# Value products ahead of the turning of probabilities in a TensorE attention stream

## The reference

```
# NSA branch, 8 heads of 64, one shared K/V group; per block of 128 queries:
s = q . k / 8 - slope * dist ;  p = softmax(s, masked) ;  o = p @ v
o_cmp  : 32 compressed keys      o_sel : all keys of the selected 64-key blocks
o_win  : the last 512 keys       o_a = g0*o_cmp + g1*o_sel + g2*o_win
# differential branch, 4 heads, two maps each:
a = softmax(s_0) - lambda * softmax(s_1) ;  o_b = a @ v      (v has 128 columns)
```

## Time and profile before

| What | Value |
|---|---|
| Median of three runs | 2092.49 us |
| Span of the profiled execution | 2086.2 us |
| PE busy in that span | 1972.7 us (95%) |
| DVE, ACT, POOL busy | 1163.0, 678.2, 152.2 us |
| Attention block in the trace | about 696 to 1106 us |

### The profile page before, as it was taken

How to read it: one execution, slowest core, us unless ns; L and a number is a source line. 1 busy time by engine, 2 the same in 40 slices (tenths; PEclk the granted TensorE clock), 3 DMA queues, 4 the chain that set the end, 5 groups by cost and what they waited for, 6 DMA issues and landing times. The chain is left out here.

```text
span 2086.2 us, 34791 instructions
## 1 busy us (share of the span) xinstructions
PE 1972.7 (95%) x13032; PEld 1856.5 (89%) x13032; DVE 1163.0 (56%) x2531; ACT 678.2 (33%) x1273; POOL 152.2 (7%) x190
## 2 busy tenths in 40 slices
PE   5889999999997799999998999999999999999997
PEld 4658798789996688898898999999999999999997
DVE  4944333334244677777775546655556565555555
ACT  5623243331223566666573133311111110101011
POOL 1442100101300100000200000000000000000000
PEclk8799999999998899999899999999999999999999
DMA  9776453521001000000003541221212020211102
GB/s 311 255 215 205 152 180 98 156 94 60 30 26 66 1 1 1 1 1 1 1 1 102 173 131 50 62 61 30 60 30 60 30 60 30 60 31 59 40 0 82
DMA packets 151758, 157.10 MB, mean 75 GB/s; under 512 B 15859, under 2 KB 132483, under 8 KB 151604
## 3 DMA queue, kind: packets, MB, share of 16 engines
q1 hardware_dynamic: 140076, 130.73, 20.4%
q0 software_dynamic: 4656, 16.40, 2.3%
q10 hardware_dynamic: 6912, 8.46, 1.1%
HBM read 139.33 MB, written 18.32 MB: 76 GB/s over the span
## 5 line engine op out<-in xcount | busy, mean ns | idle before, releaser
L1877 DVE SCALAR_TENSOR_TENSOR l_x2T<-tail_bank,g_modT,l_x2T 128x344 f32<-128x344 f32 (+1 forms) x528 | 265.3, 566 | 101.5 <-PE tail_bank L1614 101.3
L1614 PE MATMUL tail_bank<-l_wo 128*128 128x344 f32 x1584 | 270.2, 319 | 1.8 <-DVE late_total_s L1883 1.8
L1614 PEld LDWEIGHTS tail_bank<-l_wo 128*128 128x128 f32 x1584 | 252.7, 188 | 2.0 <-issue 2.0
L1448 ACT ACTIVATE l_act<-tail_bank 128x344 f32<-128x344 f32 x66 | 30.2, 457 | 523.6 <-PE tail_bank L1596 523.6
L884 PE MATMUL nsa_out<-zs_z,nsa_probT 128*128 128x64 f32 (+1 forms) x1344 | 176.1, 277 | 5.3 <-DVE zs_z L1040 5.1
L884 PEld LDWEIGHTS nsa_out<-zs_z,nsa_probT 128*128 128x128 f32 x1344 | 169.1, 198 | 7.1 <-DVE zs_z L1040 7.0
L1596 PE MATMUL tail_bank<-late_words_hi,l_uhi 128*128 128x344 f32 x528 | 169.7, 321 | 3.3 <-DVE late_words_lo L1780 3.3
L1596 PE MATMUL tail_bank<-late_words_lo,l_uhi 128*128 128x344 f32 x528 | 169.3, 321 | 0.0
L1596 PE MATMUL tail_bank<-late_words_hi,l_ulo 128*128 128x344 f32 x528 | 169.2, 320 | 0.0
L1596 PE MATMUL tail_bank<-late_words_lo,late_wo 128*128 128x344 f32 x528 | 169.1, 320 | 0.0
L1596 PE MATMUL tail_bank<-late_words_hi,l_wo 128*128 128x344 f32 x528 | 169.1, 320 | 0.0
(11 more groups left out here) (504 smaller groups left out, 4329.2 us busy)
## 6 DMA issues: line engine op xcount, KB each, us to landing
mod_wr<-in_w_ada SPq DMA_DIRECT2D x24, 1024.0 KB, 5.3
kin_kin<-in_cache_kv SPq DMA_DIRECT2D x64, 256.0 KB, 3.4
late_gate<-in_w_ffn_in SPq DMA_DIRECT2D x22, 512.0 KB, 5.7
l_raw_o<-in_w_ffn_out SPq DMA_DIRECT2D x22, 512.0 KB, 3.6
late_raw<-in_w_ffn_in SPq DMA_DIRECT2D x22, 512.0 KB, 5.4
gate_d<-dec_gate ACTq DMA_DIRECT2D x48, 172.0 KB, 2.9
late_gate<-gate_d SPq DMA_DIRECT2D x8, 1032.0 KB, 5.5
dec_vin<-in_cache_kv SPq DMA_DIRECT2D x64, 128.0 KB, 2.2
```

The costliest lines, as they stand in the source:

```text
L1448: act.activation(sg[(j + c) % 2], pg[(j + c) % 2][:, 0:TCH], ACT.Silu).then_inc(silu_done, 1)
L1614: mm = pe.matmul(po[u % 4][:, 0:TCH], w[j][:, k * P:(k + 1) * P], a[j][:, tok(c)], start=(q == 0), stop=(q == 2))
L1877: mm = dve.scalar_tensor_tensor(out=here, in0=po[u % 4][:, 0:part_w(c)], scalar=g.modT[:, 5 * KD + k, NDEC:NC9], in1=here, op0=ALU.mult, o ...
```

## The change

In `follow`, PE issues the value products of the job five back first and the turning of the job four back second. Before it was the other way round. The conditions, the waits inside both functions, the semaphores and every other engine's stream are the same.

```diff
                 def follow(t):
+                    if t >= LAG + 1:
+                        values(t - LAG - 1)
                     if LAG <= t < NJ + LAG:
                         transpose_probs(t - LAG)
-                    if t >= LAG + 1:
-                        values(t - LAG - 1)
```

## The result

The kernel after takes 2120.05 us (median of four runs, 2117.34 to 2125.08), the kernel before 2089.16 in the same set: a ratio of 1.015, interval 1.0125 to 1.0176, so 31 us slower. A second set of six runs, beside 24 of before, gave 2118.84 against 2086.88, ratio 1.0146 (1.0123 to 1.017).

What follows compares the result with a forecast made beforehand. PE (TensorE) was taken to bound the attention stage. Uncovered copies 20.0, late exponentials 4.7, `out` bank 7.8, less 1.6, 1.5 and 2, clock 0, sum to +27.4 us; on 2092.5 that gives 2120 us, range 2103 to 2138.

Steps and rivals of the forecast that it cites:

- (i): Granted clock over the attention stage: more idle time may bring more slow stretches; bounds -5 and +16 us, taken as 0.
- (a): Attention steps with a copy of four tiles or longer before a one-tile score: 13 places, together 7.9 us.
- (b): Steps with one to three tiles before a score one tile longer, and three similar: 26 places, together 7.3 us.
- (d): Drain of the attention stage: the four last jobs lose their only cover, 0.74 to 0.91 us each, 3.2 us.
- (e): ACT's in-order stream: late copies delay exponentials, and they the next copy; eight places, 4.7 us over the local loss.
- (f): Value products opening a group wait longer for DVE to free their `out` bank; fifteen places, 7.8 us net.
- (g): At the turnings, PE's wait for joined probabilities goes and longer value products hide some of DVE's copy; -1.5 us.
- (h): Score waits for DVE to empty a bank shrink as PE comes later; bounds -7.5 and 0, taken as -2 us.
- rival 3: The clock takes over: PE's added idle time pulls the clock down in more stretches; 2128 to 2137 us, chance 0.18.
- The signs: Expected in the profile after: waits for ACT's copy 25 to 30 us, L1040 some 13, PE busy 381, end near 1133.
- Hidden: Rival: job distance and slack on ACT and DVE swallow the shift in the stage; 2092 to 2100 us, chance 0.11.
- Faster: Rival: value products fill PE's waits at the turnings (L866); up to -11.5 us, about 2081, chance 0.02.

Runs made afterwards that it cites:

- e1: Kernel before, with the swap made only in the 101 steps where the remaining work still covers ACT's copy; 2089.92 us, 1.001 of before.
- e2: Kernel before, with the swap made only in the 59 steps where ACT's copy is not covered; 2119.89 us, 1.016 of before.
- e11: Kernel before, with the swap made only in 13 steps, a copy of three tiles or more before a one-tile score; 2092.25 us, 1.0024 of before.
- e4: Kernel after, with DVE's accumulation moved to the head of its close of a step; 2116.52 us, 1.0154 of before.
- e6: Kernel before, with DVE's accumulation moved to the head of its close of a step; 2082.95 us, 0.9967 of before.

## Why the prediction was right

The forecast was 2120, the medians 2120.05 and 2118.84. The sum of +27.4 us meets the 26.4 to 27.8 at full clock; the clock, put at 0 in (i), took the other 3 to 4 us, and the set of before had a median 3 us under the one it was set against. These last two cancel by chance. Inside the sum, too, some terms came out larger and some smaller than worked out, as told below, so that it meets to a microsecond is in part luck.

- **The mechanism** is shown: T(j) and V(j) with one score between them. At the first of these places the step is 0.68 longer from start to start, what (a) had; 13 such steps cost 6.6 of 7.9. In (b) 0.20 idle and 0.07 of longer products stand for 0.28. That it is local to the step was the claim behind the sum, and e1, e2 and e11 bear it out.
- **(d)** had four jobs; there are five. From the last score to the tail it takes 14.4 us in after and 9.9 in before, 4.5 and not 3.2. The miscount is mine: the last job's copy also loses V(158).
- **(e)** is only part shown. V(63) waits 0.72 us in after, where the working had 1.3: its copy comes as late as worked out, 1.6 us behind that of job 62, but V(62) waits 0.23 us itself, and this delay, which the working had in (b), also put off V(63), as I read it. Expected 4.7; not measured by itself.
- **(f)** was 7.8, less 1.6 counted twice. The wait for L1040 grew by 9.9 us, not by 8, and taking it away gave 6.6 to 8.2 at full clock in e4, of which e6, the same in before, has 1 at most. Job 146 waits 0.66 against 0.8.
- **(g)** is right: nothing waits at L866 any more.
- **(h)** did not come. The 7.5 us of score waits for L1100 that it was worked from were to shrink by 2 and shrank by 0.2; with those for L1128 and L1133 beside them the waits of L849 grew from 10.6 to 11.5. Why is not shown; I take it that the chain behind them runs through the late turning.
- **(i)** lay within its bounds: 46.6 us between 690 us and the tail at the lower level, 40.2 before, in nine stretches inside the stage where there were five. That the new short waits would bring none is not borne out, though: two of the nine, from 862.5 and from 1033.1 us, have no wait of PE over 0.61 us in the eight microseconds before them. Nor did the trace of before show the lower level only beside waits of around 2 us, as rival 3 has it (see the end).
- **The signs.** The waits for ACT's copy came to 21.3 us, not 25 to 30; those for L1040 to 15.0, where some 13 were named; the stage ends at 1139 and not near 1133. And PE's busy time in the stage did not stay at 381: of the 34 us that the stage is longer, 22 are waits and 12 are busy time. The mechanism holds, but a third of the price stands in longer matmuls. Set job by job against before, the value products are 10.3 us longer: 5.0 in the 58 groups behind a wait of over 0.1 us, 3.2 in the 81 without one, and 2.1 in the 21 that a low stretch of the clock touches in either kernel.
- **The rivals.** "Hidden" is refuted for 59 steps. For the other 101 it is true of ACT's copy (9.1 us of waits for it in e1, 7.0 before), not of the bank of `out`: e1 costs 7.1 us at full clock, adjusted 6, and that its time is only 2 to 3 us longer is partly the clock. "Faster" is refuted by the place it named: the waits of L866 went, but came back at L884. "The clock takes over" is refuted for this change (3 to 4 us), and half right for e2 and e4, where the time lies 10 to 12 us over the full-clock number (7 to 10 over the adjusted).

## What to carry to other kernels

When two groups of work swap places, count the cover for every wait from the end of the producer to the first consumer, whichever group that is; the one that comes first behind the short work pays for both. Such costs are local and add up, so swap only where the cover holds, or put one more buffer between. Compare times only beside the granted clock: a change of DVE's order (e6) that left the sum of PE's waits as it was gained 5 to 7 us, and hardly any of it at full clock.

## What the runs showed of the hardware

Three things I had not expected. First, the run-to-run spread of this kernel goes with the clock: 13.5 us of spread in time against 5 in time times clock, over 17 runs. Second, a group of value products that begins behind a wait of PE is about 0.1 us longer than before (1.08 to 1.11 us for eight, against 1.00), and the time stands in the busy time, not in the idle time. Only about half of it is the wait's: in e1 a group of eight right behind a score, with no wait, takes 1.05 us at the full clock. There the turning behind it gives about as much back, 0.36 us to the next group's start where it was 0.46. Third, a low stretch of the clock can last long behind one wait: in after PE waits 3.28 us and then runs eight products in 1.97 us, and the clock stays at 0.50 for the ten microseconds 917 to 927 (the last row of the stretches above), although PE is busy for 9.16 of them:
```profile
917.48 1.97 PE L884 MATMUL nsa_out<-zs_z,nsa_probT 128*128 128x64 f32 x8 [3.28 <-DVE zs_z L1040]
...
919.24 1.06 PE L866 MATMUL nsa_tp<-g_ident,nsa_prob 128*128 128x128 f32 x4
```
9.16 us of work at half speed are up to 4.6 us more, as an estimate, on top of the 3.3 of the wait. But a wait is not needed for it. In the profile of before the clock falls at 996.4 us behind waits of 0.67 and 0.97 us, and at 890.6 behind none: PE is busy without a gap for the ten microseconds before, the last two of them with the short score matmuls of the compressed branch.
```profile
880.00:890.00 10.00, 10.00 (x80) 9.30 (x79) 8.20 (x28) 7.57 (x20) 0.09 (x1) 1.00 0.00 0
890.00:900.00 10.00, 8.17 (x40) 7.39 (x40) 6.13 (x15) 3.94 (x10) 0.00 (x0) 0.66 0.01 2
```
The profile of e6 has a low stretch behind the same matmuls, from 888.5 us. So PE's waits alone do not tell when the level falls.
